# Encoder layer on 8 cores: weight loads spread over the steps, VectorE work put in another order, the last token blocks in parts

## The reference, cut to what matters

```python
proj = einsum('bsd,dp->bsp', x, w_in)              # gates B, C, value, pool input: 4 x 512
y_conv = gate_b * centred_short_conv(gate_c * value, conv_w)
y_pool = multiscale_pool(pool_in, pool_w, pool_scale)
mix = einsum('bsc,cd->bsd', concatenate([y_conv, y_pool]), w_out)
x = layer_norm(ALPHA * x + mix, ln1_g, ln1_b)
h = square(relu(einsum('bsd,df->bsf', x, w_ff1)))  # 1024 -> 4096
ff = einsum('bsf,fd->bsd', h, w_ff2)               # 4096 -> 1024
y = layer_norm(ALPHA * x + ff, ln2_g, ln2_b)
```

## Time and profile before

| what | value |
|---|---|
| six runs | 1265.46, 1273.64, 1278.70, 1316.01, 1346.44, 1384.74 us |
| their median | 1297.35 us |
| the profiled execution | 1278.01 us |
| its span on the slowest core (core 1) | 1276.5 us |
| spans of the cores | 1251.4 to 1276.5 us |
| TensorE matmul busy | 1156.5 us (91%) |
| VectorE busy | 934.4 us (73%) |
| GpSimd busy | 495.3 us (39%) |
| ScalarE busy | 323.9 us (25%) |

### The profile page before, as it was taken

How to read it: one execution, slowest core, us unless ns; L and a number is a source line. 1 busy time by engine, 2 the same in 40 slices (tenths; PEclk the granted TensorE clock), 3 DMA queues, 4 the chain that set the end, 5 groups by cost and what they waited for, 6 DMA issues and landing times.

```text
span 1276.5 us, 16946 instructions; the slowest of 8 cores (1251.4 to 1276.5 us)
## 1 busy us (share of the span) xinstructions
PE 1156.5 (91%) x5281; PEld 520.0 (41%) x5281; DVE 934.4 (73%) x1232; ACT 323.9 (25%) x610; POOL 495.3 (39%) x329
## 2 busy tenths in 40 slices
PE   8999999999957888999999799698898989999896
PEld 5544443444423333444444344343343434443342
DVE  2576766867836998888986577957787776787775
ACT  2422211221103333544454345311111101111110
POOL 4043432433402343343433344633455434455540
PEclk9999999999978998999999999999999989999998
DMA  9967676663796356466465698853344535433431
GB/s 152 205 124 161 187 187 162 166 206 99 183 235 192 116 162 159 150 178 177 141 175 139 170 194 174 187 182 132 132 132 157 177 121 179 158 133 132 162 118 66
DMA packets 110888, 203.12 MB, mean 159 GB/s; under 512 B 38608, under 2 KB 71504, under 8 KB 107856
## 3 DMA queue, kind: packets, MB, share of 16 engines
q1 hardware_dynamic: 97632, 170.45, 42.5%
q0 software_dynamic: 13168, 31.59, 16.4%
HBM read 149.73 MB, written 75.50 MB: 176 GB/s over the span
## 4 chain that ended last, share of the span: by engine, by line
PE 69%; DVE 11%; DMA 11%; issue 7%; ACT 1%; POOL 0%; DVEq 0%; SPq 0%; ACTq 0%; POOLq 0%
PE bank L738 51%; PE bank L331 17%; DMA scr_z<-ring_83 3%; DMA ring_86<-scr_z 2%; DMA hr_108<-scr_h 2%; DMA x1T_90<-scr_xb 1%; DMA wex<-w_ff 1%; DMA xT_64<-xet 1%; DVE st L559 1%; DMA hr_109<-scr_h 1%; DVE w_56 L342 1%; DMA ring_83<-xe 1%; DVE zs_114 L338 1%; DVE hr_108 L342 1%; DVE xbs_105 L338 1%
## 5 line engine op out<-in xcount | busy, mean ns | idle before, releaser
L331 PE MATMUL bank<-xT_64,win 128*128 128x512 bf16 (+1 forms) x608 | 113.5, 346 | 2.0 <-DMA xT_64<-xet 1.6
L335 ACT ACTIVATE sd<-mv 128x1 f32<-128x1 f32 x64 | 12.8, 201 | 394.9 <-DVE mv L561 394.9
L331 PE MATMUL bank<-xT_65,win 128*128 128x512 bf16 x512 | 111.5, 379 | 0.0
L335 ACT ACTIVATE bank<-bank 128x512 f32<-128x512 f32 x80 | 46.6, 582 | 147.2 <-PE bank L738 147.2
L331 PEld LDWEIGHTS bank<-xT_64,win 128*128 128x128 bf16 x608 | 59.0, 98 | 55.8 <-issue 4.4
L331 PEld LDWEIGHTS bank<-xT_65,win 128*128 128x128 bf16 x512 | 50.1, 98 | 59.9
L331 PE MATMUL bank<-wout,ycat_81 128*128 128x512 bf16 x256 | 57.9, 386 | 6.0 <-DVE ycat_82 L342 6.0
L331 PE MATMUL bank<-wout,ycat_82 128*128 128x512 bf16 x256 | 58.0, 387 | 5.1 <-DVE ycat_81 L342 5.1
L342 POOL TENSOR_TENSOR hst_94<-rt_102 128x512 bf16<-128x512 f32 x22 | 26.8, 1216 | 89.2 <-ACT rt_102 L335 89.2
L342 POOL TENSOR_TENSOR hst_95<-rt_101 128x512 bf16<-128x512 f32 x21 | 28.7, 1365 | 79.7 <-ACT rt_101 L335 79.7
L342 POOL TENSOR_TENSOR hst_96<-rt_103 128x512 bf16<-128x512 f32 x21 | 25.3, 1205 | 83.9 <-ACT rt_103 L335 83.9
(11 more groups left out here) (541 smaller groups left out, 3024.0 us busy)
## 6 DMA issues: line engine op xcount, KB each, us to landing
hr_108<-scr_h SPq DMA_DIRECT2D x8, 2048.0 KB, 10.0
hr_109<-scr_h SPq DMA_DIRECT2D x8, 2048.0 KB, 9.9
scr_h<-hst_94 SPq DMA_DIRECT2D x22, 512.0 KB, 3.5
scr_h<-hst_95 SPq DMA_DIRECT2D x21, 512.0 KB, 3.6
scr_h<-hst_96 SPq DMA_DIRECT2D x21, 512.0 KB, 3.5
ring_87<-scr_z SPq DMA_DIRECT2D x13, 512.0 KB, 6.4
ring_86<-scr_z SPq DMA_DIRECT2D x12, 512.0 KB, 5.4
ring_83<-xe SPq DMA_DIRECT2D x8, 512.0 KB, 10.1
```

The source lines that it names most:

```text
L331: pe.emit(lambda h: h.matmul(bank[bi][:, 0:cols], lhsT=lhsT, rhs=rhs, start=start, stop=stop), reads=reads, writes=[B_bank[bi]], signal=si ...
L335: act.emit(lambda h: h.activation(out=out, in_=in_, func=func, **kw), reads=reads, writes=writes, excl=excl)
```

## The change

In mixing, `W1[i-2].sums()` and two more calls of `pop(2)` go to the two halves of `wo`; `third` loses its sums, `fourth` its pop. Of the eleven loads of wo 6, three stay there, two go to wo 7, and six go to steps 0 to 5 of ff1. The sums in pass 0 of ff1 run one chunk closer to their use (steps 0 to 9), those of W2 one step later. In ff2, `hs1` goes behind P2, `hs2` and `hs3` behind P7, `resid` ahead of P2, and the pieces are popped singly. In block 0 the last two chunks of P1 come between chunks 13 and 14 of P5. The last block has a procedure of its own, `tail`.

```diff
         for i in range(NT - 2):
-            wo(i, i + 1, ld)
+            wo(i, i + 1, ld + [lambda: pop(2)],
+               end=[lambda i=i: (W1[i - 2].sums() if i >= 2 else None, pop(2))])
...
             def third(i=i):
                 pop(2)
-                if 1 <= i <= 5:
-                    W1[i - 1].sums()
...
             def fourth(i=i):
-                pop(2)
                 if i <= 4:
                     W1[i].load()
...
-           [lambda c=c: W1[c].load() for c in range(5, NQ)])
-        W1[5].sums()
-        wo(NT - 1, mid=[lambda: (xs1(0), xs2(0), xs3(0), xs4(0), W1[6].sums())])
+           [lambda c=c: W1[c].load() for c in range(5, 8)], end=[W1[4].sums])
+        wo(NT - 1, mid=[lambda: (xs1(0), xs2(0), xs3(0), xs4(0), W1[5].sums(), W1[8].load(), W1[9].load())])
...
             if pr == 0:
-                if q + 7 < NQ:
-                    W1[q + 7].sums()
+                if q + 6 < NQ:
+                    W1[q + 6].sums()
+                if q + 10 < NQ:
+                    W1[q + 10].load()
...
-                if q >= 2:
-                    W2[q - 2].sums()
+                if q >= 3:
+                    W2[q - 3].sums()
...
-        W2[14].sums()
-        W2[15].sums()
-
-        def ff2_prod(m, name):
+        for c in range(NQ - 3, NQ):
+            W2[c].sums()
+
+        def ff2_prod(m, name, j0=0, j1=NQ):
...
-            for j in range(NQ):
+            for j in range(j0, j1):
...
+        def tail(m):
...
+            def part(c0, c1, role):
+                bi = banks(m - 1)[role]
+                for j in range(NQ):
+                    mm(bi, c1 - c0, xap[:, j, :], W2[j].op("B21")[:, c0:c1], j == 0, j == NQ - 1,
+                       [W2[j].b["B21"], B_hr[q]], j == NQ - 1)
+                a_tt(dve, v[:, c0:c1], bank[bi][:, 0:c1 - c0], v[:, c0:c1], ALU.add, [], [B_zs[r][0]],
+                     excl=[B_bank[bi]])
+                stats(c0, c1)
+
+            pop(len(pieces))
+            upd(m, 0, 0, "X", True)
+            ff2_prod(m, "P3")
+            upd(m, 0, 1, "Z", False)
+            stats(512, 1024)
+            ff2_prod(m, "P7")
+            upd(m, 1, 1, "Y", False)
+            stats1(1)
+            ff2_prod(m, "P4")
+            upd(m, 1, 0, "Y", True)
+            stats1(0)
+            dve.emit(lambda h: h.bn_aggr(out=mv1, in_=st[2]), reads=B_st[2], writes=[B_mv2[2]])
+            ln_sqrt(2, mv1, B_mv2[2])
+            part(0, 256, "X")
+            a_stt(v1, v1, mv1[:, 0:1], gam2, ALU.subtract, ALU.mult, [B_mv2[2], B_g2], B_zs[r1])
+            ln_rstd(2, rs1, B_rstd2[2])
+            a_act(v1, v1, AF.Copy, [B_rstd2[2]], B_zs[r1], scale=rs1)
+            a_tt(pool, v1, v1, bet2, ALU.add, [B_b2], B_zs[r1])
+            load(sp, y[T * i1 + 128 * s1:T * i1 + 128 * s1 + 128, :], v1, S_zo[r1], B_zs[r1], [])
+            part(256, 384, "Y")
+            part(384, 512, "Z")
...
         for m in range(NM):
...
-            ff2_prod(m, "P1")
+            cut = NQ if m else NQ - 2
+            ff2_prod(m, "P1", 0, cut)
+            ff2_prod(m, "P5", 0, NQ - cut and cut)
+            ff2_prod(m, "P1", cut)
...
-            pop(2)
-            ff2_prod(m, "P5")
+            pop(1)
+            ff2_prod(m, "P5", NQ - cut and cut)
             upd(m, 1, 1, "Z", True)
-            if more:
-                hs1(m + 1)
             pop(1)
             ff2_prod(m, "P6")
             upd(m, 0, 1, "Y", True)
-            if more:
-                hs2(m + 1)
-                hs3(m + 1)
-                for t in range(2):
-                    resid(m + 1, t)
+            if not more:
+                tail(m)
+                break
+            pop(1)
+            for t in range(2):
+                resid(m + 1, t)
             ff2_prod(m, "P2")
             upd(m, 0, 0, "X", True)
-            pop(2)
+            hs1(m + 1)
+            pop(1)
             ff2_prod(m, "P7")
             upd(m, 1, 1, "Y", False)
+            hs2(m + 1)
+            hs3(m + 1)
             ff2_prod(m, "P3")
             upd(m, 0, 1, "Z", False)
             pieces.extend(ln2_pieces(m, 0))
-            if more:
-                hs4(m + 1)
+            hs4(m + 1)
...
             upd(m, 1, 0, "Y", True)
             pieces.extend(ln2_pieces(m, 1))
-        pop(len(pieces))
+            pop(1)
```

More of the change, by code:

```diff
@@ L986, in ln2_pieces, with stats, stats1 @@
             return [lambda: (ln_stats(v, B_zs[r], p, mv, B_mv2[p]), ln_sqrt(p, mv, B_mv2[p])), center, fin]
+        def tail(m):
+            r, q = zslot(m, 0), m % 2
+            i, s = tok(m, 0)
+            v = zs[r]
+            mv = mv2[:, 6:8]
+            rs = rstd2[:, 3:4]
+            xap = hx(q)["A12"]
+            B_st8 = [Buf(f"st8{c}") for c in range(8)]
+            r1 = zslot(m, 1)
+            i1, s1 = tok(m, 1)
+            v1, mv1, rs1 = zs[r1], mv2[:, 4:6], rstd2[:, 2:3]
+            def stats(c0, c1):
+                for c in range(c0 // 128, c1 // 128):
+                    dve.emit(lambda h, c=c: h.bn_stats(out=st8[:, 6 * c:6 * c + 6], in_=v[:, 128 * c:128 * c + 128]),
+                             reads=[B_zs[r][c // 4]], writes=[B_st8[c]])
+            def stats1(n):
+                dve.emit(lambda h: h.bn_stats(out=st[2][:, 6 * n:6 * n + 6], in_=v1[:, 512 * n:512 * n + 512]),
+                         reads=[B_zs[r1][n]], writes=[B_st[2][n]])
+            def part(c0, c1, role):
[27 more added lines that the diff above has]
+            part(384, 512, "Z")
+            dve.emit(lambda h: h.bn_aggr(out=mv, in_=st8), reads=B_st8, writes=[B_mv2[3]])
+            ln_sqrt(3, mv, B_mv2[3])
+            for n in range(2):
+                vn = v[:, 512 * n:512 * n + 512]
+                a_stt(vn, vn, mv[:, 0:1], gam2[:, 512 * n:512 * n + 512], ALU.subtract, ALU.mult,
+                      [B_mv2[3], B_g2], [B_zs[r][n]])
+            ln_rstd(3, rs, B_rstd2[3])
+            r0 = T * i + 128 * s
+            for n in range(2):
+                vn = v[:, 512 * n:512 * n + 512]
+                a_stt(vn, vn, rs, bet2[:, 512 * n:512 * n + 512], ALU.mult, ALU.add, [B_rstd2[3], B_b2], [B_zs[r][n]])
+                load(sp, y[r0:r0 + 128, 512 * n:512 * n + 512], vn, S_zo[r], [B_zs[r][n]], [])
```

## The result

| | before | after |
|---|---|---|
| median | 1273.09 us (20 runs) | 1220.91 us (10 runs) |
| ratio | | 0.9605, 95% interval 0.9576 to 0.9633 |
| profiled execution | 1278.01 us | 1217.33 us |
| spans of the cores | 1251.4 to 1276.5 us | 1202.5 to 1215.8 us |

The change makes the kernel 4% faster. From profiled to profiled execution it is 60.7 us, where 63.5 were forecast. From median to median it is 52.2; the profiled execution of before, 1278.01, lies above most of the shorter runs of before (1265 to 1279). In some executions one die shows a lower granted clock and the time is longer; the ratios, means and times of the experiments leave these out, and the changed kernel's median is then 1220.02.

What follows compares the result with a forecast made beforehand. TensorE carries the span, so time can come only from where it stands or runs at half clock. 13 + 12 - 2.5 + 7 - 2 + 35 + 1 = 63.5 off 1278.0 gives 1214.5, said as 1214 us; range 1185 to 1248.

Steps and rivals of the forecast that it cites:

- Mixing, 13: Mixing: sums and pieces leave the front of VectorE's gate, so the ycat waits go; 13 us gained, bounds 5 and 15.
- Transition, 12: Between mixing and ff1: fewer loads in the way shorten ring_83's second store, the first stays long; 12 us gained, bounds 0 and 18.
- One more sums in pass 0, -2.5: Pass 0 of ff1: ten sums instead of nine in steps that are already VectorE's; 2.5 us lost, bounds -5 and 0.
- W2's sums one step later, +7 and -2: Last ff1 pass: VectorE's wait for wex shrinks and TensorE's behind it goes, +7; later sums delay P5, -2.
- The price behind the last step, -2: End of ff1: three W2 sums instead of two behind the last step make P5 end later; -2 us, bounds -4 and +2.
- A block of ff2, 35 for 14 blocks: ff2: the block's period falls from 27.89 to 25.4 us, P4 waiting 1.0 instead of 2.3; 35 us gained, bounds 17 and 52.
- The walk: ff2: instruction-by-instruction times of one block, VectorE and GpSimd taking turns; P4 at 21.8 us, period 25.4.
- The last block, +1: ff2's last block, P2's columns last and in parts: the end comes 0 to 3 us earlier; +1, bounds -1 and +4.
- the first: Rival, ff2: centring gets in before GpSimd's first, P4 is not late, 24.3 us a block; 1199 us, chance 0.20.
- The second: Rival, transition: five loads at once keep the stores long and the 22.4 us stay; 1226 us, chance 0.13.
- the fourth: Rival, ff1: W1[10] to W1[15] land too late for their sums, stopping TensorE in six steps; slower, 1291 us, chance 0.03.
- The third: Rival, ff2: VectorE, not TensorE, sets the block's period, 27.2 us, 25 us less gain; 1239 us, chance 0.12.

Runs made afterwards that it cites:

- mix_undone: The changed kernel with mixing's sums and pieces back in the old order, all else as after: 1224.57 us, ratio 0.9642.
- tail_undone: The changed kernel with the last block of ff2 as the plain block again instead of `tail`: ratio 0.9599.
- hs1_behind: The changed kernel with ff2's hs1 moved behind P7's `upd`, instead of in front of the later finish: 1203.71 us, ratio 0.9469.

## Why the prediction was right, and where it was not

The time was right: 1214 said, 1220.91 the median, 1217.33 the profiled execution. That the sum came so close is in part luck. On core 1 the last pass was worth 8 us less than said (-1.1, where +7 was forecast), and passes 1 and 2 of ff1, for which the forecast has no term, lost 3.0; mixing, transition and blocks gave 2.4, 2.4 and 3.9 more than said and made up for most of it. And core 1 is the slowest core: in the mean over cores the spans fell by 52.2 us (1262.1 to 1209.9). Term by term, on core 1, on which the forecast was read:

- *Mixing, 13:* 15.4 on core 1, 10.7 in the mean. The mechanism is shown: the ycat waits go with this edit alone and come back with its undoing. Its worth to the whole is less, 4.5 us by mix_undone: some 3 us come back in ff1 in the profiled executions, and the rest of the way from 10.7 to 4.5 no run explains. The forecast reckoned as if what comes later stayed put.
- *Transition, 12:* 14.4 on core 1, 12.9 in the mean; undone 12.3 in the mean. The steps were right one by one: five loads together, the first store still long (16.76), the second under 6 (5.6), w_52 near 27 (24.4).
- *One more sums in pass 0, -2.5:* the rest of pass 0 took 3.7 us longer on core 1. That the sums are the cause was not tested by themselves.
- *W2's sums one step later, +7 and -2:* **the step that failed**. "VectorE then waits 2.5, less than the ... 2.8 that cost nothing before" is true of wex (1.47), but VectorE stood again right behind it, for a store that was late with the same load. Core 1 lost 1.1 us over the last pass (the mean over six cores with whole records gained 0.8), and undoing it is 3.5 us faster. The forecast also read the wait of 5.7 on z_99 on the core where it was longest; over the eight cores TensorE's waits in that part of the pass were 4.27 us before and 5.23 after. What should have been asked is why wex was late: something in front held the engines, and that something had other customers. The price behind the last step, -2, was of the right size (P5's wait from 4.85 to 6.13 in the mean over cores), the gain was not there to pay it.
- *A block of ff2, 35 for 14 blocks:* 38.9 us for blocks 1 to 14 on core 1 (34.7 for the 13 that the earlier trace rows spans), 33.0 in the mean, undone 30.2. The walk came out nearly to the tenth. From P1 at 903.04: Z's upd 7.18 (said 7.2), GpSimd 11.00 (11.0), centring 11.32 and behind GpSimd (11.3), P4 21.76 (21.8) after a wait of 0.88 (1.0). In between, too: X's upd ended at 15.03 (15.0), hs1 at 17.73 (17.7), the finish at 21.01 (21.0). The period is 25.21 (25.4). That a wait of 1.0 costs no half clock held too: every block of the chain took 24.35.
- *The last block, +1:* 0.4 on core 1, and 0.4 by tail_undone.

The rule of the Trainium skill ("SBUF — State Buffer", section "Who interferes with whom") that such instructions of VectorE and GpSimd exclude each other is borne out here: 3.12, 2.77 and 3.36 us with GpSimd at work, 1.27, 1.22 and 1.28 without it.

Of the rivals, the first, that P4's wait goes wholly when centring gets in before GpSimd, was not what this change did, but it is what hs1_behind did: 24.17 us a block against the 24.3 named. The second (the pacing does not pace) and the fourth (sums wait on loads) fell: paced loads land in 5.6 to 9.7 us. The third (VectorE sets the period) fell: VectorE is busy 22.96 of 25 us in the changed kernel, near to it, but hs1_behind does the same work of VectorE in 24.17.

## What to carry to other kernels

A wait on a late transfer should be followed to what holds the transfer before the waiting work is put off: here, put off, it met the next late thing, and came due elsewhere. Where two engines exclude each other, the lengths in the profile hold their waiting, and it can be enough to move one instruction behind the point that the bottleneck waits for: that gave the same block of 24.17 us as freeing all of them from the turns. When several operands come out of one series of subtractions, it is worth trying to make them in the order in which the products ask for them.

## What was not expected of the hardware

- Four subtractions of 128x512 in bf16 took 1.81 us alone, 2.46 to 3.31 with GpSimd's short squares beside them, and 8.72 beside its four multiply/adds of 1024 columns.
- Fractions of a microsecond went with who came first: with GpSimd 0.32 us ahead of VectorE's centring three instructions of VectorE in front of P4 were stretched by 1.6 to 2.1 us each, with VectorE 0.67 us ahead none there was.
- The first row store of the transition hardly minds how many loads stand in GpSimd's queue (18.0 and 18.5 us with eleven, 16.8 and 15.5 with five, 15.4 with four); the second fell from 15 to 5.6.
